# Attention by head pairs: two heads' scores on the two row halves of TensorE, their outputs on the two column halves, and VectorE on both heads at once

## The chip, the cores and the metric

The kernel runs on one core of one Trainium2 chip. The metric is the time of one execution on the device in microseconds. Three runs of the kernel before gave a median of 1569.54 us (1569.21 to 1569.62).

## The reference

Two model blocks are applied to 256 tokens of width 1024: the first has a gated-mixing layer, an attention layer and two feed-forward layers, the second three mixers and a mixture of 32 experts. The change touches only the attention core of the first block, with 16 heads of 64 elements. In the reference it is a softmax over three dilated patterns, merged by their log-sum-exp:

```python
for window, dilation in DILATED_PATTERNS:
    o, lse = dilated_branch(q, k, v, window, dilation)
...
wts = jax.nn.softmax(jnp.stack(lses, axis=0), axis=0)
return jnp.einsum('pbsh,pbshd->bshd', wts, jnp.stack(outs, axis=0))
```

For 256 tokens this equals one causal softmax whose score for a query and key has the logarithm of the number of patterns that hold the pair added to it, and that is how the kernel computes it: scores times 1/8 plus a table (`bias`), row maximum, exponential, sum, division, product with the values.

## The kernel before, in words

Tokens lie along the free axis, features on the partitions. There are two blocks of 128 query rows. The first sees 128 keys, the second all 256, so one head has 128 x 384 scores: a part c=0 of 128 columns and a part c=1 of 256. `qk1` holds queries and keys with two heads per tile, the even head on partitions 0 to 63 and the odd one on 64 to 127.

Each engine has its own program, in a fixed order written out by hand, and semaphores join them. In the attention loop (PE L990 to L1019, ScalarE L1574 to L1590, VectorE L2088 to L2112) each pass i deals with one head at different depths:

- PE: scores of head i (L996 and L997, into `mixbank(i)`, two PSUM banks in turn), after waiting until VectorE has read the scores of head i-2. After every odd head, one step of an unrelated vector-matrix product (`modulation`, L900: four matmuls of 512 columns, each on its own 32 columns of the array). Then three transposes of the probabilities of head i-2 (L1007), then three output matmuls of head i-3 (L1016 to L1018), whose 64 output rows lie on partition half i % 2 of `lin`.
- VectorE: scale and bias of head i (L2093), two row maxima (L2097), then reciprocal (L2102) and two multiplications (L2104) for head i-1, and in every even pass the split of a finished pair's outputs into `r_hi` and `r_lo` (`split_rows`, L1872 and L1873).
- ScalarE: two exponentials with their sums for head i (L1580), then the copy of the transposed probabilities of head i-2 from PSUM (L1588).

A VectorE pass i waits for outputs up to head i-3. PE computes these in its own pass i, ahead of which it needs the probabilities of head i-2, and those VectorE made in pass i-1, one pass earlier.

The loop starts when the last values are copied (L2084) and ends where `project` (L1022) multiplies all eight tiles of `r_hi` and `r_lo` by the output weights (L692 to L694). One `w_lo` split of a weight panel (L1848) stands in VectorE's order between the last two `split_rows`.

Of the kernel before, what the change touches and what calls it, by code (L numbers as in the profile page):

```python
# [24 lines left out]
ALU = mybir.AluOpType  # L25
ACT = mybir.ActivationFunctionType
AX = mybir.AxisListType.X
ds = bass.ds

P = 128  # L30
T = 256
NT = T // P
# [7 lines left out]
HEADS = 16  # L40
HD = 64
# [21 lines left out]
OUT1 = QKV1 + 3 * KD  # L63
# [119 lines left out]
def program(nc, A, out):  # L183
# [3 lines left out]
    with ctx:  # L187
# [27 lines left out]
        K, at = {}, 0  # L215
# [42 lines left out]
        lin = [ctx.enter_context(nc.psum_tensor(f"lin{b}", [P, 512], F32)) for b in range(4)]  # L258
        stat = ctx.enter_context(nc.psum_tensor("stat", [P, 4, T], F32))
        mixp = ctx.enter_context(nc.psum_tensor("mixp", [P, 4, T], F32))  # L260
# [41 lines left out]
        scores_ready = sem("scores_ready")  # L302
        scores_read = sem("scores_read")
        max_ready = sem("max_ready")
        exp_ready = sem("exp_ready")
        probs_ready = sem("probs_ready")
        pt_ready = sem("pt_ready")
        pt_copied = sem("pt_copied")
        o_ready = sem("o_ready")
        o_copied = sem("o_copied")  # L310
# [63 lines left out]
        low, a = Arena(moe_low, MOE_LOW), Arena(moe_high, MOE_HIGH)  # L374
# [82 lines left out]
        a = Arena(mixers_t, MIXERS)  # L457
# [12 lines left out]
        a = Arena(mixers_t, MIXERS)  # L470
        qk1 = a.take(16 * T).rearrange("p (k t) -> p k t", k=16)
# [4 lines left out]
        vt1 = a.take(NT * D).rearrange("p (c f) -> p c f", c=NT)  # L476
        SC = 3 * P
        s1 = a.take(4 * SC).rearrange("p (b s) -> p b s", b=4)
# [8 lines left out]
        def statbank(n):  # L487

            return stat[:, 2 * (n % 2):2 * (n % 2) + 2, :].rearrange("p a t -> p (a t)")

        def mixbank(n):

            return mixp[:, 2 * (n % 2):2 * (n % 2) + 2, :].rearrange("p a t -> p (a t)")
# [170 lines left out]
        def _(pe):  # L664
# [229 lines left out]
            def modulation(bank, first, count):  # L894

                for a in range(first, first + count):
                    k = a % KD
                    pe.wait_ge(ada_loaded[a % ARING], 16 * (a // ARING + 1))
                    for q in range(4):
                        mm = pe.matmul(bank[32 * q:32 * q + 32, :], c_act[:, k:k + 1].to_broadcast([P, 32]),  # L900
                                       aring[:, a % ARING, q * 512:(q + 1) * 512], start=k == 0, stop=k == KD - 1,
                                       skip_group_check=True)
                    mm.then_inc(ada_done, 1)
# [83 lines left out]
                mm.then_inc(vt1_ready, 1)  # L987
            pe.wait_ge(vt1_copied, 4)
            pe.wait_ge(qk_ready, 16)
            for i in range(HEADS + 3):  # L990
                if i < HEADS:
                    if i >= 2:
                        pe.wait_ge(scores_read, i - 1)
                    o = 64 * (i % 2)
                    q, k = qk1[o:o + 64, i // 2, :], qk1[o:o + 64, 8 + i // 2, :]
                    pe.matmul(mixbank(i)[:, 0:P], q[:, 0:P], k[:, 0:P], start=True, stop=True, skip_group_check=True)  # L996
                    pe.matmul(mixbank(i)[:, P:3 * P], q[:, P:T], k, start=True, stop=True, skip_group_check=True)\  # L997
                        .then_inc(scores_ready, 1)
                if i < HEADS and i % 2 == 1:
                    modulation(lin[2], 16 + i // 2, 1)  # L1000
                if 2 <= i <= HEADS + 1:
                    g = i - 2
                    pe.wait_ge(probs_ready, g + 1)
                    if g >= 2:
                        pe.wait_ge(pt_copied, g - 1)
                    for c in range(3):
                        mm = pe.transpose(statbank(g)[:, c * P:(c + 1) * P], p1[:, g % 4, c * P:(c + 1) * P], K["ident"])  # L1007
                    mm.then_inc(pt_ready, 1)
                if i >= 3:
                    g = i - 3  # L1010
                    pe.wait_ge(pt_copied, g + 1)
                    if g >= 4 and g % 2 == 0:
                        pe.wait_ge(o_copied, g // 2 - 1)
                    o = lin[(g // 2) % 2][64 * (g % 2):64 * (g % 2) + 64, :]
                    v = [vt1[:, c, g * HD:(g + 1) * HD] for c in range(NT)]
                    pe.matmul(o[:, 0:P], v[0], pt1[:, g % 4, 0:P], start=True, stop=True, skip_group_check=True)  # L1016
                    pe.matmul(o[:, P:T], v[0], pt1[:, g % 4, P:2 * P], start=True, stop=False, skip_group_check=True)
                    pe.matmul(o[:, P:T], v[1], pt1[:, g % 4, 2 * P:3 * P], start=False, stop=True, skip_group_check=True)\  # L1018
                        .then_inc(o_ready, 1)  # L1019
            pe.wait_ge(o_copied, 8)  # L1020
            pe.wait_ge(modrow_ready, 3)
            project((r_hi, r_lo))  # L1022
# [376 lines left out]
        def _(act):  # L1399
# [10 lines left out]
            def split_hi(upto):  # L1410

                for n in range(next_split[0], upto):
                    next_split[0] = n + 1
                    if is_split(n):
                        act.wait_ge(panel_loaded[n % RING], 16 * (n // RING + 1))
                        act.wait_ge(panel_done, n - RING + 1)
                        act.activation(w_hi[:, n % RING, :], ring[:, n % RING, :], ACT.Copy).then_inc(w_hi_ready, 1)  # L1417
# [152 lines left out]
            for n in range(8):  # L1570
                panels.done()
                panels.advance(1)
                split_hi(panels.n + RING)
            for i in range(HEADS + 2):  # L1574
                if i < HEADS:
                    act.wait_ge(max_ready, i + 1)
                    if i >= 4:
                        act.wait_ge(pt_ready, i - 3)
                    for c, (a0, a1) in enumerate(((0, P), (P, 3 * P))):
                        ins = act.activation(p1[:, i % 4, a0:a1], s1[:, i % 4, a0:a1], ACT.Exp,  # L1580
                                             bias=mx1[:, 2 * i + c:2 * i + c + 1], accum_out=l1[:, 2 * i + c:2 * i + c + 1])
                    ins.then_inc(exp_ready, 1)
                if i >= 2:
                    g = i - 2
                    act.wait_ge(pt_ready, g + 1)
                    if g >= 4:
                        act.wait_ge(o_ready, g - 3)
                    act.activation(pt1[:, g % 4, :], statbank(g)[:, 0:SC], ACT.Copy).then_inc(pt_copied, 1)  # L1588
                    if i == HEADS:
                        split_hi(OUT1 + 1)  # L1590
            split_hi(OUT1 + 4)
            modulation_row(lin[2][:, :], 2)
            stream_norm()
# [230 lines left out]
        def _(dve):  # L1824
# [3 lines left out]
            def link(ins):  # L1828

                ins.then_inc(dve_step, 1)  # L1830
                dve.wait_ge(dve_step, seen(dve_step))
# [38 lines left out]
            def split_rows(tiles, src):  # L1870

                link(dve.tensor_copy(r_hi[:, tiles, :], src))  # L1872
                return dve.tensor_tensor(r_lo[:, tiles, :], src, r_hi[:, tiles, :].bitcast(F32), ALU.subtract)  # L1873
# [211 lines left out]
            a0 = list(K).index("bias00")  # L2085
            bias_at = sum(v.shape[1] for v in list(consts.values())[:a0])
            bias = cst[:, bias_at:bias_at + SC]
            for i in range(HEADS + 3):  # L2088
                if i < HEADS:
                    dve.wait_ge(scores_ready, i + 1)  # L2090
                    if i >= 4:
                        dve.wait_ge(exp_ready, i - 3)
                    dve.scalar_tensor_tensor(s1[:, i % 4, :], mixbank(i)[:, 0:SC], HD ** -0.5, bias, ALU.mult, ALU.add)\  # L2093
                        .then_inc(scores_read, 1)
                    dve.wait_ge(scores_read, i + 1)
                    for c, (a0, a1) in enumerate(((0, P), (P, 3 * P))):
                        ins = dve.tensor_reduce(mx1[:, 2 * i + c:2 * i + c + 1], s1[:, i % 4, a0:a1], AX, ALU.max, negate=True)  # L2097
                    ins.then_inc(max_ready, 1)
                if 1 <= i <= HEADS:
                    g = i - 1  # L2100
                    dve.wait_ge(exp_ready, g + 1)
                    link(dve.reciprocal(r1[:, 2 * g:2 * g + 2], l1[:, 2 * g:2 * g + 2]))  # L2102
                    for c, (a0, a1) in enumerate(((0, P), (P, 3 * P))):
                        ins = dve.tensor_scalar(p1[:, g % 4, a0:a1], p1[:, g % 4, a0:a1], r1[:, 2 * g + c:2 * g + c + 1],  # L2104
                                                None, ALU.mult)
                    ins.then_inc(probs_ready, 1)
                if i >= 4 and i % 2 == 0:
                    j = (i - 4) // 2
                    dve.wait_ge(o_ready, 2 * j + 2)
                    split_rows(j, lin[j % 2][:, 0:T]).then_inc(o_copied, 1)  # L2110
                if i == HEADS + 1:
                    split_lo(OUT1 + 1)  # L2112
            split_lo(OUT1 + 4)
            residual(8)
# [498 lines left out]
```

## Time and profile before

| what | value |
|---|---|
| median of three runs | 1569.54 us |
| span of the profiled execution, first to last instruction | 1563.5 us |
| difference of the two | 6.0 us |
| PE busy over the span | 95% |
| VectorE, ScalarE, GpSimd busy | 50%, 37%, 19% |
| mean granted TensorE clock | 0.977 |
| attention loop, first score matmul to first matmul of `project` | 430.18 to 473.98 us |

The profile gives no total of its own for the profiled execution; the 6.0 us are what a median run has outside such a span. PE's busy share is modelled from its instructions and includes the time in which a half or a quarter of the array works. A granted clock of 1.00 is 2.4 GHz, 0.50 is 1.2 GHz.

### The profile page before, as it was taken

Reading aid. Unit: us, or ns where it says so; the run is one execution under the profiler, and the core shown is the slowest. Engines: PE = TensorE matmul, PEld = TensorE weight load, DVE = VectorE, ACT = ScalarE, POOL = GpSimd, SP = SyncE. Lnnn points to the kernel's source line nnn. Section 1 sums busy time; section 2 is a strip of 40 time slices with the busy share of each in tenths; the row PEclk is TensorE's granted clock in tenths of the full one; section 3 lists DMA queues with packets and bytes.
Section 4 is the critical chain, followed back from the end, with each engine's and each line's share of the span. In section 5 each row is a group of like instructions: output and inputs, shape, how many; then the busy total and the mean of one; then the engine's idle time right before and its main releaser. Section 6 shows DMA issues by size and latency. Waiting matters only on the chain.

```text
span 1563.5 us, 28411 instructions
## 1 busy us (share of the span) xinstructions
PE 1478.1 (95%) x11270; PEld 1234.4 (79%) x11270; DVE 777.1 (50%) x1404; ACT 573.0 (37%) x927; POOL 294.7 (19%) x121
## 2 busy tenths in 40 slices
PE   7978999999999999999999998999899999998997
PEld 5857999999958999999999887999566666555554
DVE  4964888648584888634463532572422222221122
ACT  2345545444354655437663113634211111111111
POOL 0021222212201112225763000684000000000000
PEclk9989999999999999998999996999999999999999
DMA  8674455565434555643543210476999999999996
GB/s 310 238 277 153 167 165 171 195 235 162 136 135 135 171 181 176 210 149 108 175 137 96 80 55 14 149 269 233 423 424 423 425 427 425 426 425 424 427 424 262
DMA packets 72097, 375.82 MB, mean 240 GB/s; under 512 B 8128, under 2 KB 8384, under 8 KB 49984
## 3 DMA queue, kind: packets, MB, share of 16 engines
q1 hardware_dynamic: 72000, 374.43, 63.5%
q8 instruction: 73, 1.20, 0.3%
q14 instruction: 24, 0.20, 0.0%
HBM read 373.35 MB, written 1.05 MB: 239 GB/s over the span
## 4 chain that ended last, share of the span: by engine, by line
PE 64%; issue 13%; DVE 8%; DMA 8%; SPq 5%; ACT 2%; POOL 1%; POOLq 0%; DVEq 0%; ACTq 0%
PE lin L692 9%; PE lin L694 8%; PE lin L693 8%; DMA moe_low<-in_experts 6%; PE stat L1376 5%; PE mixp L1349 4%; PE mixp L1353 4%; DVE mixers L2011 3%; SPq L609 3%; PE lin L711 2%; PE stat L1309 2%; PE lin L1319 1%; DMA moe_high<-in_experts 1%; PE stat L692 1%; PE stat L693 1%
## 5 line engine op out<-in xcount | busy, mean ns | idle before, releaser
L692 PE MATMUL lin<-r_hi,w_hi 128*128 128x256 f32 x1464 | 427.2, 292 | 12.0 <-POOL w_lo L1815 5.1
L693 PE MATMUL lin<-r_lo,w_hi 128*128 128x256 f32 x1464 | 417.4, 285 | 0.0
L694 PE MATMUL lin<-r_hi,w_lo 128*128 128x256 f32 x1464 | 417.3, 285 | 0.0
L692 PEld LDWEIGHTS lin<-r_hi,w_hi 128*128 128x128 f32 x1464 | 284.2, 194 | 19.6 <-POOL w_lo L1815 6.7
L693 PEld LDWEIGHTS lin<-r_lo,w_hi 128*128 128x128 f32 x1464 | 284.2, 194 | 0.8
L694 PEld LDWEIGHTS lin<-r_hi,w_lo 128*128 128x128 f32 x1464 | 284.1, 194 | 0.0
L1819 POOL TENSOR_TENSOR w_lo<-ring,w_hi 128x1024 fp32r<-128x1024 f32 x71 | 175.5, 2484 | 217.9 <-ACT w_hi L1417 217.7
L1815 POOL TENSOR_TENSOR w_lo<-ring,w_hi 128x1024 fp32r<-128x1024 f32 x42 | 108.2, 2577 | 481.5 <-ACT w_hi L1423 298.3
L1848 DVE TENSOR_TENSOR w_lo<-ring,w_hi 128x1024 fp32r<-128x1024 f32 x126 | 156.4, 1245 | 84.8 <-ACT w_hi L1423 65.1
L1423 ACT ACTIVATE w_hi<-ring 128x1024 fp32r<-128x1024 f32 x124 | 129.7, 1049 | 57.3 <-PE mixp L694 49.3
L1417 ACT ACTIVATE w_hi<-ring 128x1024 fp32r<-128x1024 f32 x119 | 124.0, 1050 | 33.8 <-PE lin L694 16.7
L2519 DVE TENSOR_TENSOR moe_low<-moe_low,mixp 128x256 f32<-128x256 f32 x32 | 13.5, 421 | 207.4 <-ACT moe_low L1789 207.4
L711 PE MATMUL lin<-h,ring 128*128 128x256 f32 x400 | 91.0, 385 | 3.0 <-DVE h L1879 3.0
L1789 ACT ACTIVATE moe_low<-mixp 128x256 f32<-128x256 f32 x32 | 12.3, 384 | 221.7 <-PE mixp L1353 221.7
L711 PEld LDWEIGHTS lin<-h,ring 128*128 128x128 f32 x400 | 76.1, 193 | 16.9 <-issue 6.7
L2526 DVE SCALAR_TENSOR_TENSOR e_y_lo<-stat,moe_high,e_y_hi 128x512 fp32r<-128x512 f32 x32 | 24.0, 751 | 117.3 <-ACT e_y_hi L1794 117.3
L1376 PE MATMUL stat<-moe_high,moe_low 128*64 128x512 f32 x352 | 80.4, 598 | 0.0
L1505 ACT ACTIVATE sgf<-ub 128x256 f32<-128x256 f32 x44 | 18.4, 418 | 119.0 <-DVE ub L1930 119.0
L1349 PE MATMUL mixp<-moe_low,h 128*64 128x256 f32 x352 | 53.3, 381 | 6.9 <-DMA moe_low<-in_experts 4.2
L1349 PE MATMUL mixp<-moe_low,cat 128*64 128x256 f32 x352 | 53.3, 381 | 5.9 <-DMA moe_high<-in_experts 3.5
L1376 PEld LDWEIGHTS stat<-moe_high,moe_low 128*64 128x64 f32 x352 | 23.2, 136 | 40.7 <-issue 37.8
L2011 DVE SCALAR_TENSOR_TENSOR mixers<-mixers,colp 128x256 f32<-128x256 f32 x120 | 53.9, 514 | 0.9
(482 smaller groups left out, 2773.7 us busy)
## 6 DMA issues: line engine op xcount, KB each, us to landing
ring<-in_panels SPq DMA_DIRECT2D x272, 512.0 KB, 3.9
moe_low<-in_experts SPq DMA_DIRECT2D x64, 1024.0 KB, 22.9
moe_high<-in_experts SPq DMA_DIRECT2D x22, 2048.0 KB, 24.9
aring<-in_ada SPq DMA_DIRECT2D x24, 1024.0 KB, 6.0
ring<-in_experts SPq DMA_DIRECT2D x20, 1024.0 KB, 26.9
moe_high<-in_experts SPq DMA_DIRECT2D x20, 1024.0 KB, 22.1
cst<-in_experts SPq DMA_DIRECT2D x10, 1280.0 KB, 23.8
sq<-in_experts SPq DMA_DIRECT2D x10, 1024.0 KB, 29.4
```

Source lines behind the costliest of these rows:

```text
L692: pe.matmul(o, w_hi[:, slot, c], r[0], start=start, stop=False, skip_group_check=True)
L693: pe.matmul(o, w_hi[:, slot, c], r[1], start=False, stop=False, skip_group_check=True)
L694: return pe.matmul(o, w_lo[:, slot, c], r[0], start=False, stop=stop, skip_group_check=True)
L711: mm = pe.matmul(lin[b][:, 0:T], w[:, i, :], rhs[:, i, :], start=i == 0, stop=i == k - 1)
L1349: pe.matmul(o[:, 0:T], lhs, gate_weights(slot, k)[:, half * T:(half + 1) * T], start=k == 0, stop=k == KD - 1, skip_group_check=True)
L1376: mm = pe.matmul(statbank(1)[64 * half:64 * half + 64, :], e_hidT[:, k % 2, k // 2, :], down_weights(slot, k, half), start=k == 0, stop=k ...
L1417: act.activation(w_hi[:, n % RING, :], ring[:, n % RING, :], ACT.Copy).then_inc(w_hi_ready, 1)
L1423: act.activation(w_hi[:, n % RING, :], ring[:, n % RING, :], ACT.Copy).then_inc(w_hi_ready, 1)
L1815: pool.tensor_tensor(w_lo[:, POOL_SLOT, :], ring[:, POOL_SLOT, :], w_hi[:, POOL_SLOT, :].bitcast(F32), ALU.subtract).then_inc(w_split_pool, 1)
L1819: pool.tensor_tensor(w_lo[:, n % RING, :], ring[:, n % RING, :], w_hi[:, n % RING, :].bitcast(F32), ALU.subtract).then_inc(w_split_pool, 1)
L1848: dve.tensor_tensor(w_lo[:, n % RING, :], ring[:, n % RING, :], w_hi[:, n % RING, :].bitcast(F32), ALU.subtract)\
L2011: ins = dve.scalar_tensor_tensor(cv0[:, j, :], hc0[:, j, tap:tap + T], w, cv0[:, j, :], ALU.mult, ALU.add)
```

## The change

PE, ScalarE and VectorE now take a pair of heads per pass, in nine or ten passes instead of 18 or 19.

- Scores: `score_pair(j)` issues c=0 of both heads, then c=1 of both, so that consecutive matmuls use the two halves of the array's rows and two PSUM banks. One pair fills both banks, and the next pair waits until VectorE has read them. `score_pair(j + 1)` stands first in PE's pass j, then `modulation`, then the six transposes of pair j-1, then the outputs of pair j-2.
- Outputs: for each of the three products both heads are issued one after the other, on the two column halves.
- VectorE: one scale-and-bias of 128 x 768, two maxima over both heads, one reciprocal of four columns, and two multiplications of both heads by a broadcast reciprocal (`tensor_tensor` in place of `tensor_scalar`). Pass j ends with `split_rows` of pair j-2, which waits for that pair's outputs.
- ScalarE: the same instructions, in pairs.
- The buffers stay at four heads, that is two pairs.

The removed lines are those of the kernel above; they are left out here.

```diff
--- before.py
+++ after.py
@@ -987,36 +987,46 @@
                 mm.then_inc(vt1_ready, 1)
             pe.wait_ge(vt1_copied, 4)
             pe.wait_ge(qk_ready, 16)
...
+            def score_pair(j):
+                if j:
+                    pe.wait_ge(scores_read, j)
+                for part in range(2):
+                    for n in range(2):
+                        q, k = (qk1[64 * n:64 * n + 64, t, :] for t in (j, 8 + j))
+                        if part == 0:
+                            pe.matmul(mixbank(n)[:, 0:P], q[:, 0:P], k[:, 0:P], start=True, stop=True, skip_group_check=True)
+                        else:
+                            mm = pe.matmul(mixbank(n)[:, P:3 * P], q[:, P:T], k, start=True, stop=True, skip_group_check=True)
+                mm.then_inc(scores_ready, 1)
+            score_pair(0)
+            for j in range(HEADS // 2 + 2):
+                if j + 1 < HEADS // 2:
+                    score_pair(j + 1)
+                if j < HEADS // 2:
+                    modulation(lin[2], 16 + j, 1)
+                if 1 <= j <= HEADS // 2:
+                    g = j - 1
                     pe.wait_ge(probs_ready, g + 1)
+                    for n in range(2):
+                        if g:
+                            pe.wait_ge(pt_copied, 2 * g - 1 + n)
+                        for c in range(3):
+                            mm = pe.transpose(statbank(n)[:, c * P:(c + 1) * P], p1[:, 2 * (g % 2) + n, c * P:(c + 1) * P], K["ident"])
+                        mm.then_inc(pt_ready, 1)
+                if j >= 2:
+                    g = j - 2
+                    pe.wait_ge(pt_copied, 2 * g + 2)
                     if g >= 2:
...
+                        pe.wait_ge(o_copied, g - 1)
                     for c in range(3):
...
+                        for n in range(2):
+                            head = 2 * g + n
+                            o = lin[g % 2][64 * n:64 * n + 64, (0 if c == 0 else P):(P if c == 0 else T)]
+                            mm = pe.matmul(o, vt1[:, c // 2, head * HD:(head + 1) * HD],
+                                           pt1[:, 2 * (g % 2) + n, c * P:(c + 1) * P], start=c < 2, stop=c != 1, skip_group_check=True)
+                    mm.then_inc(o_ready, 1)
             pe.wait_ge(o_copied, 8)
             pe.wait_ge(modrow_ready, 3)
             project((r_hi, r_lo))
@@ -1571,23 +1581,27 @@
                 panels.done()
                 panels.advance(1)
                 split_hi(panels.n + RING)
...
+            for j in range(HEADS // 2 + 1):
+                if j < HEADS // 2:
+                    act.wait_ge(max_ready, j + 1)
+                    if j >= 2:
+                        act.wait_ge(pt_ready, 2 * j - 2)
+                    for n in range(2):
+                        at = 2 * (j % 2) + n
+                        for c, (a0, a1) in enumerate(((0, P), (P, 3 * P))):
+                            m = 2 * (2 * j + n) + c
+                            ins = act.activation(p1[:, at, a0:a1], s1[:, at, a0:a1], ACT.Exp, bias=mx1[:, m:m + 1],
+                                                 accum_out=l1[:, m:m + 1])
                     ins.then_inc(exp_ready, 1)
...
+                if j:
+                    g = j - 1
+                    for n in range(2):
+                        act.wait_ge(pt_ready, 2 * g + n + 1)
+                        if g >= 2:
+                            act.wait_ge(o_ready, g - 1)
+                        act.activation(pt1[:, 2 * (g % 2) + n, :], statbank(n)[:, 0:SC], ACT.Copy).then_inc(pt_copied, 1)
+                if j == HEADS // 2 - 1:
+                    split_hi(OUT1 + 1)
             split_hi(OUT1 + 4)
             modulation_row(lin[2][:, :], 2)
             stream_norm()
@@ -2085,30 +2099,38 @@
             a0 = list(K).index("bias00")
             bias_at = sum(v.shape[1] for v in list(consts.values())[:a0])
             bias = cst[:, bias_at:bias_at + SC]
...
+            scores = mixp[:, :, :].rearrange("p (n a) t -> p n (a t)", n=2)[:, :, 0:SC]
+            def per_row(ap, j, c):
+                return ap[:, 4 * j:4 * j + 4].rearrange("p (n c) -> p n c", c=2)[:, :, c]
+            for j in range(HEADS // 2 + 2):
+                if j < HEADS // 2:
+                    pair = slice(2 * (j % 2), 2 * (j % 2) + 2)
+                    dve.wait_ge(scores_ready, j + 1)
+                    if j >= 2:
+                        dve.wait_ge(exp_ready, j - 1)
+                    dve.scalar_tensor_tensor(s1[:, pair, :], scores, HD ** -0.5, bias.unsqueeze(1).broadcast_to([P, 2, SC]),
+                                             ALU.mult, ALU.add).then_inc(scores_read, 1)
+                    dve.wait_ge(scores_read, j + 1)
                     for c, (a0, a1) in enumerate(((0, P), (P, 3 * P))):
...
+                        ins = dve.tensor_reduce(per_row(mx1, j, c), s1[:, pair, a0:a1], AX, ALU.max, negate=True)
                     ins.then_inc(max_ready, 1)
...
+                if 1 <= j <= HEADS // 2:
+                    g = j - 1
+                    pair = slice(2 * (g % 2), 2 * (g % 2) + 2)
                     dve.wait_ge(exp_ready, g + 1)
...
+                    link(dve.reciprocal(r1[:, 4 * g:4 * g + 4], l1[:, 4 * g:4 * g + 4]))
                     for c, (a0, a1) in enumerate(((0, P), (P, 3 * P))):
...
+                        ins = dve.tensor_tensor(p1[:, pair, a0:a1], p1[:, pair, a0:a1],
+                                                per_row(r1, g, c).unsqueeze(2).broadcast_to([P, 2, a1 - a0]), ALU.mult)
                     ins.then_inc(probs_ready, 1)
...
+                if j >= 2:
+                    g = j - 2
+                    dve.wait_ge(o_ready, g + 1)
+                    split_rows(g, lin[g % 2][:, 0:T]).then_inc(o_copied, 1)
+                if j == HEADS // 2:
                     split_lo(OUT1 + 1)
             split_lo(OUT1 + 4)
             residual(8)
```

## Rows read from the trace of the kernel before

**Rows 1.** Stretch, length, busy of PE, PEld, DVE, ACT, POOL, granted clock, DMA share, GB/s.

```profile
445.00:450.00 5.00, 5.00 (x35) 2.82 (x32) 4.00 (x14) 2.72 (x10) 0.00 (x0) 1.00 0.55 193
```

**Rows 2.** The chain of waits over one period of two heads: start, length, what.

```profile
440.84 0.99 PE lin L900 x8
441.84 0.48 PE stat L1007 x3
442.31 0.36 PE lin L1016 x2
442.68 0.22 PE lin L1017 x2
...
443.11 0.42 PE mixp L996 x2
443.53 0.43 PE mixp L997 x2
...
446.09 0.99 PE lin L900 x8
```

**Rows 3.** Timeline of PE: eight transposes, two heads' scores, first `project` matmul.

```profile
426.72 1.07 PE L985 MATMUL mixp<-cst,mixers 128*128 128x128 f32 x8 [0.56 <-issue]
...
430.18 0.50 PE L996 MATMUL mixp<-mixers 64*128 64x128 f32 x4 [0.78 <-DVE mixers L2084]
430.50 0.61 PE L997 MATMUL mixp<-mixers 64*128 64x256 f32 x4
...
473.98 0.39 PE L692 MATMUL lin<-r_hi,w_hi 128*128 128x256 f32 x1 [0.98 <-DVE r_lo L1873]
```

**Rows 4.** Timeline of VectorE: start, length, line; one head, then a split.

```profile
435.17 0.15 DVE L2102 RECIPROCAL mixers<-mixers 128x2 f32<-128x2 f32 x1
...
435.36 0.55 DVE L2104 TENSOR_SCALAR mixers<-mixers 128x128 f32<-128x128 f32 x2
...
435.82 0.55 DVE L2093 SCALAR_TENSOR_TENSOR mixers<-mixp,cst 128x384 f32<-128x384 f32 x1
436.41 0.61 DVE L2097 TENSOR_REDUCE mixers<-mixers 128x1 f32<-128x128 f32 x2
...
436.94 0.16 DVE L2102 RECIPROCAL mixers<-mixers 128x2 f32<-128x2 f32 x1
...
440.53 0.42 DVE L1872 CAST r_hi<-lin 128x256 fp32r<-128x256 f32 x1
...
440.98 0.42 DVE L1873 TENSOR_TENSOR r_lo<-lin,r_hi 128x256 fp32r<-128x256 f32 x1
```

**Rows 5.** VectorE by line and shape, whole run: count, busy us, mean ns, idle before.

```profile
L2375 DVE SCALAR_TENSOR_TENSOR arena<-stat,arena 128x768 f32<-128x768 f32 x1 | 0.9, 950 | 0.0
L2231 DVE TENSOR_TENSOR arena<-arena 128x512 f32<-128x512 f32 x2 | 1.3, 686 | 0.0
L2097 DVE TENSOR_REDUCE mixers<-mixers 128x1 f32<-128x256 f32 x16 | 6.5, 409 | 0.0
L2097 DVE TENSOR_REDUCE mixers<-mixers 128x1 f32<-128x128 f32 x16 | 4.6, 286 | 0.6
```

**Rows 6.** Timeline of PE in later stages: three matmul groups that followed an idle time (in brackets).

```profile
869.79 1.28 PE L1170 MATMUL stat<-cst,arena 128*128 128x128 f32 x8 [2.22 <-DVE arena L2296]
...
935.19 1.89 PE L1217 MATMUL mixp<-arena 64*128 64x128 f32 x8 [0.85 <-DVE arena L2333]
...
1425.51 0.65 PE L1349 MATMUL mixp<-ring,h 128*64 128x256 f32 x4 [1.69 <-DMA modrow<-in_experts]
```

**Rows 7.** Granted clock (third number from the end) around those three.

```profile
870.00:871.00 1.00, 1.00 (x9) 1.00 (x8) 1.00 (x2) 0.00 (x0) 0.00 (x0) 0.78 0.00 0
935.00:936.00 1.00, 0.81 (x4) 0.81 (x5) 0.14 (x1) 0.00 (x0) 0.00 (x0) 0.71 0.00 0
1420.00:1430.00 10.00, 8.31 (x80) 5.29 (x80) 1.11 (x2) 1.07 (x2) 0.00 (x0) 1.00 1.02 420
940.00:950.00 10.00, 7.86 (x30) 6.57 (x30) 1.81 (x5) 0.00 (x0) 0.00 (x0) 0.50 0.01 2
```

More of the change, by code:

```diff
@@ L989, in _ @@
             pe.wait_ge(qk_ready, 16)
[L990 to L1002, printed above, removed]
-                    pe.wait_ge(probs_ready, g + 1)
+            def score_pair(j):
[9 more added lines that the diff above has]
+                mm.then_inc(scores_ready, 1)
@@ L1004, in _ @@
                     if g >= 2:
-                        pe.wait_ge(pt_copied, g - 1)
+                        pe.wait_ge(o_copied, g - 1)
                     for c in range(3):
[L1007 to L1019, printed above, removed]
+                        for n in range(2):
[3 more added lines that the diff above has]
+                                           pt1[:, 2 * (g % 2) + n, c * P:(c + 1) * P], start=c < 2, stop=c != 1, skip_group_check=True)
@@ L1573, in _ @@
                 split_hi(panels.n + RING)
[L1574 to L1581, printed above, removed]
-                    ins.then_inc(exp_ready, 1)
[L1583 to L1590, printed above, removed]
+            for j in range(HEADS // 2 + 1):
[9 more added lines that the diff above has]
+                                                 accum_out=l1[:, m:m + 1])
+                    ins.then_inc(exp_ready, 1)
+                if j:
[7 more added lines that the diff above has]
+                    split_hi(OUT1 + 1)
             split_hi(OUT1 + 4)
@@ L2087, in _ @@
             bias = cst[:, bias_at:bias_at + SC]
[L2088 to L2095, printed above, removed]
+            scores = mixp[:, :, :].rearrange("p (n a) t -> p n (a t)", n=2)[:, :, 0:SC]
@@ L2096, in _ @@
                     for c, (a0, a1) in enumerate(((0, P), (P, 3 * P))):
-                        ins = dve.tensor_reduce(mx1[:, 2 * i + c:2 * i + c + 1], s1[:, i % 4, a0:a1], AX, ALU.max, negate=True)
+                        ins = dve.tensor_reduce(per_row(mx1, j, c), s1[:, pair, a0:a1], AX, ALU.max, negate=True)
                     ins.then_inc(max_ready, 1)
-                if 1 <= i <= HEADS:
-                    g = i - 1
+                if 1 <= j <= HEADS // 2:
+                    g = j - 1
+                    pair = slice(2 * (g % 2), 2 * (g % 2) + 2)
@@ L2101, in _ @@
                     dve.wait_ge(exp_ready, g + 1)
-                    link(dve.reciprocal(r1[:, 2 * g:2 * g + 2], l1[:, 2 * g:2 * g + 2]))
+                    link(dve.reciprocal(r1[:, 4 * g:4 * g + 4], l1[:, 4 * g:4 * g + 4]))
                     for c, (a0, a1) in enumerate(((0, P), (P, 3 * P))):
-                        ins = dve.tensor_scalar(p1[:, g % 4, a0:a1], p1[:, g % 4, a0:a1], r1[:, 2 * g + c:2 * g + c + 1],
-                                                None, ALU.mult)
+                        ins = dve.tensor_tensor(p1[:, pair, a0:a1], p1[:, pair, a0:a1],
+                                                per_row(r1, g, c).unsqueeze(2).broadcast_to([P, 2, a1 - a0]), ALU.mult)
@@ L2106, in _ @@
                     ins.then_inc(probs_ready, 1)
[L2107 to L2111, printed above, removed]
+                if j >= 2:
[3 more added lines that the diff above has]
+                if j == HEADS // 2:
```

## The prediction

> **What bounds the kernel now.** I read the chain of waits over the attention loop first. It runs through PE alone, with the same pieces in every period of two heads, 440.84 to 446.09, that is 5.25 us: one `modulation` at 0.99, then twice (transposes 0.48, outputs 0.36 + 0.22 + 0.22 = 0.80, scores 0.42 + 0.43 = 0.85) [rows 2]; 0.99 + 2 x 2.13 = 5.25. The busy times by stretch say the same: PE 5.00 of 5.00 us, VectorE 4.00, ScalarE 2.72, clock 1.00 [rows 1]. A product of 128 columns takes 0.22 once the array streams; the first of a group takes 0.36 or 0.42, so each change from one tile shape to the next costs 0.14 to 0.21. The `modulation` row shows that column tiles already work side by side: four matmuls of 512 columns in 0.99 us, where one after the other, at 0.43 for 256 columns, they would need 3.4. The row halves do too: two heads' scores together ran from 430.18 to 431.11, 0.93 us, where their columns add up to 2 x 0.65 [rows 2, 3].
>
> **PE's own work after.** Per pair: scores 0.21 + 0.22 + 0.43, about 0.85; `modulation` 0.99; six transposes, by eight that took 1.07 [rows 3], 0.86; outputs 0.80. Sum 3.50 instead of 5.25. Two thirds of the saving is the second head riding along (1.3), the rest fewer changes of shape.
>
> **VectorE's own work after.** Where no wait lies between, an instruction starts 0.09 before the previous one's end (0.55 long, the next after 0.46), and after a semaphore 0.04 to 0.05 behind it [rows 4].
> - Scale and bias over 768 elements: 0.95 by a row of that shape [rows 5], plus 0.05: 1.00.
> - Maxima: from 286 to 409 ns for 128 more elements [rows 5], so 0.41 for 256 and 0.65 for 512 elements; start to next start 0.32 + 0.57 = 0.89 (two heads singly: 2 x 0.53).
> - Reciprocal to multiplication: 0.19 [rows 4], taken as 0.20.
> - Multiplications. No row shows one with a broadcast factor. The old form takes 0.55 for both parts of one head; a `tensor_tensor` takes 0.42 for 256 and 0.69 for 512 elements [rows 4, 5], which gives 0.33 + 0.69 = 1.02 to the end. That is the value I take. Bounds: the slope of the old form would give about 0.73, twice one head 1.10.
> - Split: copy to subtraction 0.45, subtraction 0.42 less 0.09 [rows 4]: 0.78 before the next can start.
>
> Together 3.8 us per pair (0.94 for the multiplications when nothing waits on their end), hardly less than the 2 x 1.79 + 0.78 = 4.4 of before. If both engines only had to do their work, the period would be 3.8.
>
> **The added wait.** But VectorE's pass j ends with the split of pair j-2, whose outputs PE computes in its pass j behind the transposes of pair j-1, and these need the multiplications of VectorE's same pass j. Before, the probabilities came from one pass earlier, so that slack is gone. Queued behind the waiting split are the scale of pair j+1, the maxima, and so ScalarE's exponentials, and PE's scores of pair j+2, whose banks that scale has to free. So the two engines take turns:
>
> 1.00 (scale) + 0.89 (maxima) + 0.20 (reciprocal) + 1.02 (multiply, to its end) + 0.05 + 0.86 (six transposes) + 0.80 (outputs) + 0.04 + 0.78 (split) = 5.64 us per pair, against 5.25.
>
> What hides: scores and `modulation`, 0.85 + 0.99 from 0.05 after the scale, end at 2.9 and the probabilities come at 3.1. ScalarE's exponentials (2 x 0.9) and two copies (0.9), 2.7 in all by its busy time per period [rows 1], fit behind the maxima and ahead of the next outputs. Bounds of the cycle: transposes 0.80 to 0.97, the multiplications as above, 5.3 to 5.9.
>
> **Whole loop at full clock.** Scores from 430.18, scale 0 at 431.04, scale 1 at 432.9 (its banks), scale 2 at 436.1 (waits for the exponentials, 1.9 us, then multiplies; no split yet), scale 3 at 441.8 (first full cycle), then 5.64 each: scale 7 at 464.3. Split of pair 5 ends at 469.9; multiplications 7 end 471.1; transposes and outputs of pair 6 until 472.9, its split until 473.7; the `w_lo` split that stands there 1.1; last split 0.87; `project` starts about 475.8, against 473.98 [rows 3]. That is +1.8 us: the first passes win what the later cycles lose. The move of `w_hi` work on ScalarE costs nothing, since its engine is idle half the time [rows 1]. The later stages follow unchanged, and so do the 6.0 us that a median run has outside the span of the profiled one.
>
> **The clock.** Before, PE never rested in the loop and the clock stayed at 1.00. After, from the end of the outputs to the next scores PE rests for split + scale, 0.04 + 0.78 + 1.00 + 0.05 = 1.9 us, in each of the five full cycles, and another 0.2 ahead of the transposes. In this trace a rest of 1.69 us between dense groups left the clock at 1.00, one of 2.22 was followed by 0.50 (the row of 870 shows 0.78, the change within it), and so were two of 0.85 close together among small matmuls on half the rows or columns, at 935; that stretch then stayed at 0.50 for about 30 us [rows 6, 7]. A rest of 1.9 every 5.6 us, with small matmuls between, resembles these more than the first. I take it that the clock falls to 1.2 GHz. The Trainium skill, "TensorE: Matmul & The Clock Gate", section on a second failure mode, says that a kernel that idles briefly between groups of matmuls while it cycles through PSUM makes the clock swing between its two levels; by that rule too the clock falls, where the rests alone would not decide.
>
> Price at 1.2 GHz: scores and `modulation` grow by 0.64 + 0.85 and end at 4.4, so the transposes wait 1.3 longer; transposes and outputs grow by 0.6 + 0.6. A cycle at the low clock costs 2.5 more, 8.1. At the low clock PE is busier and should win the clock back, then lose it again; I take half of the five full cycles, 2.5 x 2.5 = 6.2. `project` may begin at the low clock, which I leave within the range (a few us of dense work at half rate). Sum: 1.8 + 6.2 = +8.0, so 1577.5.
>
> A rule that speaks against the change is in the skill's "TensorEngine Tiling (Array Packing)", section on the PSUM bottleneck: tiling speeds up TensorE but not the reading of PSUM. The trace agrees: VectorE's 3.8 above PE's 3.5.
>
> **Rivals.**
> - The clock holds at 2.4 GHz. For: 1.9 is nearer to 1.69 than to 2.22, and PE is busy for two thirds of the cycle. Against: the fall at 935 with shorter rests. Time 1569.5 + 1.8 = 1571.3 (1569 to 1574). 28%.
> - Faster: VectorE doesn't wait for the outputs, and its 3.8 us set the pace. This needs the split to find its outputs done; it decides once transposes and outputs are finished when the multiplications end. Seven periods would save 7 x (5.25 - 3.8) = 10, so 1559.5. Against it stands PE's written order. 5%.
> - The clock falls and does not come back, as after 935 [rows 7]. All five cycles at +2.5, the first and last passes and the opening of `project` some 4 more: 1.8 + 12.5 + 4, so 1588. 8%.
> - The change does not do what it says: halves don't run side by side when issued alternately. Outputs +0.64, and scores +0.64 of which 0.4 shows, 1.0 a cycle, 1.8 + 7 x 1.0, so 1578. Against: rows 2 and 3. 4%.
>
> **How the numbers follow.** Forecast 55%, own range 1573 to 1583. Less than 0.2%, 3.1 us, can't be told from no change. Faster than that: the second rival and a hair of the first, 6%. Within it: most of the first rival and the low end of the forecast, 27%. Slower 67%. The range reaches down over the first rival and up short of the third: 1569.5 to 1584.
>
> **What would show it.** VectorE's wait before the split's copy should be released by PE's outputs, some 1.75 us in each pass from the third on, and PE's before the scores by the scale, 1.9 us. The period should be 5.6 at clock 1.00 and about 8 at 0.50; the granted clock of 440 to 475 says which case holds. Outputs of a pair in 0.8 us show the column halves side by side. The forecast is wrong if that clock stays at 1.00, or if the split finds its outputs ready.

## The result and the profile after

The changed kernel took 1576.56 us (median of 4 runs, 1575.65 to 1577.92) against 1569.58 us for the kernel before (also 4 runs); the ratio is 1.0047, 95% interval 1.0033 to 1.0061. It is slower, 0.9 us from the forecast of 1577.5. The profiled execution took 1575.65 us with a span of 1573.9 us, so 1.8 us lie outside the span, not the 6.0 taken before.

From the first score matmul (431.34) to the first matmul of `project` (484.19) the attention loop took 52.9 us, against 43.8 [rows 3]: 9.1 us more, while the medians differ by 7.0. Loops are compared this way below, because what lies ahead of and behind the loop is not the same in every execution: span less loop was 1515.4 us in one profile of this document (e8) and 1524.9 in another (e5), and 1519.7 before and 1521.0 after the change. The 2 us between 9.1 and 7.0 are within that and stay unexplained.

These two lines stand at the head of the changed kernel's page; VectorE is busy a little less than before (777.1 us), although the kernel is longer:

```profile
span 1573.9 us, 28344 instructions
...
PE 1473.2 (94%) x11270; PEld 1229.4 (78%) x11270; DVE 771.7 (49%) x1356; ACT 573.1 (36%) x927; POOL 295.3 (19%) x121
```

The chain of waits over one period of two heads, the answer to [rows 2]: start, length, what.

```profile
449.31 0.44 DVE r_hi L1886
449.80 0.31 issue
450.11 0.96 DVE mixers L2114
451.11 0.49 PE mixp L998 x4
451.60 0.76 PE mixp L1000 x4
452.36 1.86 PE lin L900 x8
454.23 1.19 PE stat L1016 x6
455.42 0.83 PE lin L1027 x12
456.27 0.43 DVE r_hi L1886
```

The chain was PE alone; now it passes from VectorE (split, scale) to PE (scores, `modulation`, transposes, outputs) and back, in 456.27 - 449.31 = 6.96 us instead of 5.25. `modulation` takes 1.86 instead of 0.99, though it is the same eight instructions. The stretches of one us say why (behind the bounds and the length stands PE's busy time; the granted clock is the third number from the end):

```profile
449.00:450.00 1.00, 0.26 (x6) 0.01 (x2) 0.66 (x2) 0.00 (x0) 0.00 (x0) 1.00 0.90 369
450.00:451.00 1.00, 0.00 (x0) 0.00 (x0) 1.00 (x2) 0.00 (x0) 0.00 (x0) 1.00 0.95 401
451.00:452.00 1.00, 0.89 (x8) 0.54 (x8) 0.97 (x3) 0.00 (x0) 0.00 (x0) 0.79 0.32 131
452.00:453.00 1.00, 1.00 (x6) 0.20 (x8) 0.97 (x4) 0.86 (x4) 0.00 (x0) 0.50 0.00 0
453.00:454.00 1.00, 1.00 (x8) 0.00 (x0) 0.25 (x1) 1.00 (x6) 0.00 (x0) 0.50 0.00 0
454.00:455.00 1.00, 1.00 (x8) 0.84 (x5) 0.00 (x0) 0.00 (x0) 0.00 (x0) 0.51 0.00 0
455.00:456.00 1.00, 1.00 (x16) 0.81 (x14) 0.00 (x0) 0.87 (x2) 0.00 (x0) 1.00 0.74 98
```

PE rests from 449.26 to 451.11, works again, and is put to 1.2 GHz (0.50) within the same us; it returns to 2.4 GHz while the transposes run. Four full periods in a row look like this; the one ahead of them, from scale to scale 443.14 - 437.40 = 5.74 us, ran wholly at 1.00:

```profile
437.40 0.95 DVE L2114 SCALAR_TENSOR_TENSOR mixers<-mixp,cst 128x768 f32<-128x768 f32 x1
...
443.14 0.95 DVE L2114 SCALAR_TENSOR_TENSOR mixers<-mixp,cst 128x768 f32<-128x768 f32 x1
```

The timeline has the rest as an idle time in brackets, and VectorE's wait for the outputs:

```profile
451.11 0.49 PE L998 MATMUL mixp<-mixers 64*128 64x128 f32 x4 [1.85 <-DVE mixers L2114]
```

```profile
449.31 0.42 DVE L1886 CAST r_hi<-lin 128x256 fp32r<-128x256 f32 x1 [3.02 <-PE lin L1027]
```

### The profile page after: what moved, and what is told of

The parts are those of the page before. It is cut to its first block, busy times and chain, and to the rows that moved or that the text cites. A ratio compares the mean times of both kernels' runs of the same rounds, so it can differ in the third digit from the quotient of the medians.

```text
span 1573.9 us, 28344 instructions
## 1 busy us (share of the span) xinstructions
PE 1473.2 (94%) x11270; PEld 1229.4 (78%) x11270; DVE 771.7 (49%) x1356; ACT 573.1 (36%) x927; POOL 295.3 (19%) x121
## 4 chain that ended last, share of the span: by engine, by line
PE 61%; issue 13%; DVE 9%; DMA 7%; SPq 7%; ACT 2%; POOL 1%; POOLq 0%; DVEq 0%; ACTq 0%
PE lin L692 8%; PE lin L694 8%; PE lin L693 8%; DMA moe_low<-in_experts 5%; PE stat L1386 4%; PE mixp L1359 4%; PE mixp L1363 4%; SPq L609 3%; DVE mixers L2025 3%; PE lin L711 2%; PE stat L1319 2%; DMA moe_high<-in_experts 1%; PE lin L1329 1%; PE stat L692 1%; PE mixp L692 1%
```

## The experiments

Each experiment was measured in turn with the kernel before, whose median was 1569.3 us beside e1 to e4, 1569.2 beside e5 to e8, 1569.4 beside e9 to e11 and 1569.6 beside the changed kernel; each ratio is to its own one. The loop runs from the first score matmul to the first matmul of `project`; the period is the time per pair of heads in the middle of the loop. Both come from the one profiled execution of each kernel.

| kernel | median us | ratio, 95% interval | loop us | period us |
|---|---|---|---|---|
| before | 1569.3 | 1 | 43.8 | 5.25 |
| changed | 1576.6 | 1.0047 (1.0033 to 1.0061) | 52.9 | 6.96 |
| e1 fill | 1572.0 | 1.0023 (1.0009 to 1.0037) | 46.3 | 5.72 |
| e2 late split | 1556.3 | 0.9911 (0.9898 to 0.9924) | 33.2 | 3.85 |
| e3 modulation last | 1569.8 | 1.0001 (0.9989 to 1.0012) | 48.6 | 5.72, 7.06 |
| e4 fill, head by head | 1573.4 | 1.0033 (1.0017 to 1.0049) | 48.7 | 5.98 |
| e5 old kernel, added wait | 1577.1 | 1.0046 (1.0028 to 1.0064) | 54.3 | 6.48 |
| e6 late split, ScalarE rounds | 1551.8 | 0.9877 (0.9858 to 0.9896) | 31.7 | 3.47 |
| e7 late split, VectorE single | 1559.0 | 0.9930 (0.9916 to 0.9944) | 34.5 | 4.02 |
| e8 late split, PE head by head | 1557.3 | 0.9918 (0.9904 to 0.9931) | 33.9 | 3.85 |
| e9 = e6 again | 1555.5 | 0.9890 (0.9867 to 0.9913) | 31.7 | 3.47 |
| e10 = e6, PE head by head | 1556.5 | 0.9910 (0.9894 to 0.9927) | 33.3 | 3.74 |
| e11 = e6, VectorE single | 1556.1 | 0.9910 (0.9887 to 0.9933) | 32.5 | 3.55 |

**e1, the rest filled.** Behind the outputs of passes 2 to 6:

```diff
+                    if j < HEADS // 2 - 1:
+                        for _ in range(3):
+                            pe.matmul(lin[3][:, 0:T], K["ident"], cst[:, 0:T], ...)
```

> The changed kernel with three extra matmuls of 256 columns (about 1.3 us, into a bank nobody reads) behind the outputs of passes 2 to 6, where TensorE rests 1.9 us. Theory (VectorE and TensorE take turns at 5.6 us a pair, and the rest of 1.9 us drops the clock, which adds 1.3 us a pair): clock 1.00 in the whole loop, period 5.6 us instead of 6.97, about 1569.6 + 1.8 = 1571.4 us. Rival 1 (the low clock only goes along with the loss, the period is long for another reason): period near 7, 1576.5 us as before the fill. Rival 2 (the turn-taking costs nothing at full clock): period 5.25 or less, 1569.5 us or below.

The clock stayed at 1.00 from 430 to 484 and the period is 5.72. The chain of waits over one period:

```profile
449.93 0.43 DVE r_hi L1889
450.42 0.31 issue
450.73 0.96 DVE mixers L2117
451.71 1.01 DVE mixers L2121 x2
452.84 1.04 DVE mixers L2129 x2
453.92 0.88 PE stat L1016 x6
454.80 0.83 PE lin L1027 x12
455.65 0.43 DVE r_hi L1889
```

This is the turn-taking by itself: split, scale, maxima, multiplications, transposes, outputs, each engine idle while the other works. Extra work made the kernel faster by 6.6 us in the loop and 4.6 in the median; the intervals of the two ratios overlap at their ends, so the loop carries this verdict. Rival 1 is out, and so is rival 2, since 5.72 is above 5.25 and the interval above 1. The 12 runs spread from 1567.9 to 1578.7; the last passes have no fill, and one profile can't show whether the clock falls there in some executions.

**e2, the wait removed.** VectorE splits pair j-3 in pass j:

```diff
-            for j in range(HEADS // 2 + 2):
+            for j in range(HEADS // 2 + 3):
...
-                if j >= 2:
-                    g = j - 2
+                if j >= 3:
+                    g = j - 3
```

> The changed kernel with VectorE's split of a pair's outputs one pass later (pair j-3 in pass j, one pass more), so that it no longer waits for outputs that depend on its own pass's multiplications. Theory (the added wait makes the two engines take turns): the wait is gone, VectorE's work of 3.8 us sets the period, TensorE rests too little for the clock to fall, and the loop ends some 10 us before that of the old kernel: 1559.5 us (1557 to 1562). Rival 1 (PSUM banks and transposed copies form the next cycle at once): period 4.5 to 5.2, 1563 to 1569 us. Rival 2 (the loss came from the pairing itself, wide VectorE instructions and tile changes): no gain over the changed kernel, 1574 to 1577 us.

VectorE no longer waits; the chain is VectorE alone, 452.49 - 448.64 = 3.85 us a pair, as its work was summed (3.8), and the clock is 1.00 throughout the loop. The loop is 10.6 us shorter than the old one (10 expected), the median 13.0 shorter. Both rivals fail.

```profile
448.64 0.96 DVE mixers L2114
449.62 1.01 DVE mixers L2118 x2
450.75 1.03 DVE mixers L2126 x2
451.78 0.34 DVE r_hi L1886
452.18 0.31 issue
452.49 0.96 DVE mixers L2114
```

**e3, the long rest cut in two.** `modulation` moved behind the outputs:

```diff
+                if j < HEADS // 2:
+                    modulation(lin[2], 16 + j, 1)
```

> The changed kernel with the modulation step moved from behind the scores to the end of TensorE's pass, into the long rest. The rest of 1.9 us becomes one of 0.9 us, and one of about 1.2 us opens ahead of the transposes; the work and VectorE's turn-taking stay. If the clock falls for one long rest, it now stays at 1.00 and the time is that of the filled kernel, about 1571.5 us. If it falls for the sum of rests within a few us, it falls as before; the modulation then runs at the low clock off the path, so the period is 6 to 7 us and the time 1574 to 1577 us.

Neither answer came out clean. Four of the five full periods kept 1.00 and took 5.72 us, one took 7.06, and the clock also fell in an early pass and in the last ones; the runs spread from 1564.7 to 1574.1, and the profiled one is at the slow end. The fall in the middle of the loop came behind two short rests:

```profile
457.98 0.49 PE L998 MATMUL mixp<-mixers 64*128 64x128 f32 x4 [0.85 <-DVE mixers L2114]
458.30 0.60 PE L1000 MATMUL mixp<-mixers 64*128 64x256 f32 x4
460.17 1.11 PE L1014 MATMUL stat<-cst,mixers 128*128 128x128 f32 x4 [1.27 <-DVE mixers L2126]
```

```profile
460.00:461.00 1.00, 0.83 (x4) 0.83 (x5) 0.11 (x1) 0.87 (x4) 0.00 (x0) 0.54 1.04 442
```

So no single long rest is needed; rests of 0.85 and 1.27 us with 0.9 us of matmuls between were followed by a fall once, and the same pattern one period earlier was not. The median, 1569.8, lies below the 1571.5 expected for a clock that holds; no profile shows why.

**e4, outputs head by head at full clock.** e1 with the loops over c and n swapped.

> The filled kernel with the outputs head by head (three products of the even head, then three of the odd one) instead of alternating between the column halves. Theory (halves overlap between neighbouring matmuls alone): five slots of 0.21 us instead of three, +0.43 us a pair on the path, outputs 1.25 us, about 3 us over the filled kernel. Rival (the queue overlaps the halves however they are ordered): no difference. Rival (nothing overlaps in this order): 1.45 us, +0.64 a pair, about 5 us over.

Outputs took 1.09 us instead of 0.83, less than the 1.25 expected: +0.26 a pair, period 5.98. The median is 1.4 us above e1 with intervals that overlap; the loop is 2.4 longer, 1.6 of it by 0.26 in each of six passes and the rest in the last passes, where the clock fell (0.50 from 477.1 to 480.5 in this profile).

```profile
454.77 1.09 PE lin L1027 x12
```

**e5, the added wait alone, in the old kernel.**

```diff
-                if i >= 4 and i % 2 == 0:
-                    j = (i - 4) // 2
+                if i >= 3 and i % 2 == 1:
+                    j = (i - 3) // 2
```

> The kernel before, one head a pass and everything as it was, with only VectorE's split of a finished pair moved one pass earlier (odd passes from the third), so that it waits for outputs that need the probabilities of its own pass: the added wait alone, without pairs. Theory (the wait is what costs): VectorE's 4.4 us for two heads plus a wait for three transposes and three outputs, 0.05 + 0.5 + 0.8, and some time lost when TensorE in its turn waits for scales: 5.7 to 6.2 us per two heads instead of 5.25, 1573 to 1577 us if the clock holds, more if it falls. Rival (the loss belongs to the paired form): period 5.25, 1569.3 us.

No pair, no wide instruction, no alternation, and the same loss: 1577.1 us, period 457.15 - 450.67 = 6.48. The period is longer than expected, since the outputs also wait for ScalarE's copies, which stand behind its exponentials; and it is at clock 1.00 (450 to 460), so here the wait costs by itself, in the median, what in the changed kernel wait and clock cost together. The profiled execution took 1581.0 us, and its loop is 10.5 us longer than the old one. The edit has a side effect at the end: the `w_lo` split now stands behind the last `split_rows`, PE rests 2.31 us ahead of `project`, and that began at 0.50 (488 to 491), so a part of this profile's loss lies behind the loop.

```profile
449.87 0.43 DVE r_hi L1872
450.37 0.31 issue
450.67 0.56 DVE mixers L2093
451.25 0.62 DVE mixers L2097 x2
...
452.21 0.68 ACT mixers L1580 x3
452.89 0.38 ACT mixers L1588
453.31 0.43 PE lin L1016 x2
...
457.15 0.56 DVE mixers L2093
```

**e6 and e9, ScalarE takes the rounding.** e2 with the copy to `r_hi` on ScalarE, ahead of the exponentials of its pass:

```diff
+                if j >= 3:
+                    g = j - 3
+                    act.wait_ge(o_ready, g + 1)
+                    act.activation(r_hi[:, g, :], lin[g % 2][:, 0:T], ACT.Copy).then_inc(v_scaled, 1)
```

> The kernel with the late split, with ScalarE making the rounded upper part of the outputs ahead of its exponentials, VectorE only the subtraction. If VectorE's work is the bound of that kernel (3.85 us a pair), its 0.45 us less bring the period to TensorE's 3.5 to 3.6 us and the time 1.5 to 2 us below the late split, about 1554.5 us. Rival (the chain scale, maxima, exponentials, multiplications is the bound): the added 0.45 us on ScalarE delays the exponentials and the time is the same or up to 2 us longer.

> The kernel with the late split and ScalarE's share once more, since its first four runs lay far apart (1548.5 to 1557.7). If its gain is the shorter loop (31.7 us from the first scores to the projection in its profile, against 43.8), the median comes out near 1569.3 - 12.1 = 1557; if more than the loop is gained, near 1552 again.

PE alone is on the chain again, 450.37 - 446.90 = 3.47 us a pair, the 3.5 summed for its work (profile of e9):

```profile
446.90 0.42 PE mixp L998 x4
447.32 0.43 PE mixp L1000 x4
447.76 0.99 PE lin L900 x8
448.75 0.81 PE stat L1016 x6
449.56 0.81 PE lin L1027 x12
450.37 0.42 PE mixp L998 x4
```

The loop is 12.1 us shorter than the old one in both profiles. The medians are 17.4 and 13.9 us lower, with intervals that overlap; the ten runs of both together have a median of 1553.8 us, 15.5 lower. What goes beyond the loop's 12.1 is not explained: the two fastest runs of e9 (1547.5 and 1548.5) had a mean granted clock of 0.981 and 0.982, its others 0.975 to 0.978, so the spread is in part one of the clock elsewhere. Against e2 the loop gains 1.5 us; the medians of e2 and e9, 0.9 apart, don't separate them. Its loop is the shortest of all, and it is ahead of both given kernels.

**e7 and e8, one part of the change taken out of e2.** e7: two scales, four maxima and four TENSOR_SCALAR multiplications per pair. e8: scores and outputs head by head within the pass.

> The kernel with the late split, with VectorE's scale, maxima and multiplications head by head again (two, four and four instructions of the old shapes, TENSOR_SCALAR for the multiplication), TensorE in pairs. It takes away only the third part of the change, both heads at once on VectorE. By the rows of the old kernel the work grows from 3.85 to about 4.05 us a pair: +1.5 us in all, about 1558 us. If wide instructions were what makes the late split fast, the period would go back towards 4.4 or 5.2, 1561 to 1567 us.

> The kernel with the late split, with the scores and the outputs issued head by head within the pass instead of alternately: takes away only the alternation. TensorE's work grows by 0.13 (scores) and 0.26 (outputs, as in the filled kernel) to 3.9 us a pair, just VectorE's 3.85: same time or up to 1.5 us more, 1556 to 1558 us. If neighbouring matmuls on opposite halves are what gives the speed, outputs at 1.44 and scores at 1.28: 4.6 us a pair, 1562 us.

In e7 a pair takes 4.02 us instead of 3.85, and the loop 1.3 more: wide VectorE instructions are worth 0.17 us a pair where VectorE is the bound. Its median is 2.6 above e2's, with intervals that overlap. In e8 the period is the same and the median 0.9 higher, which can't be told from no change: in the steady period the alternation is worth nothing where VectorE is the bound. The outputs took 0.26 longer as expected, but the scores no longer, where 0.13 had been expected. The loop is 0.6 longer; in this profile the clock was at 0.50 from 430.5 to 433.9, in the first passes, where in e2 it was not, and what each of the two did to those 0.6 can't be told apart.

**e10 and e11, the same two parts taken out of e6**, where PE is the bound.

> The same kernel with scores and outputs head by head within a pass. TensorE sets its period (3.47 us), so here the alternation must show where it works: outputs 1.07 instead of 0.81 and scores the same, 3.7 us a pair, +2 us in all. If alternation did nothing: no change. If the halves overlap only when alternated (scores too): 3.47 + 0.64 + 0.43 = 4.5, +7 us.

> The same kernel with VectorE head by head (old shapes). VectorE's work is 3.85 - 0.45 + 0.16 = 3.6 us a pair by the profiles of the late-split kernels, TensorE's 3.47: +0.1 us a pair, within 1 us of the kernel with pairs. If the wide instructions matter more: +0.5 us a pair, +4 us.

In e10 a pair takes 3.74 us and the loop 1.6 more. All but 0.01 of the 0.27 a pair is in the outputs (1.07 against 0.81); the scores take 0.43 + 0.43 against 0.42 + 0.43. In e11 a pair takes 3.55 us and the loop 0.8 more. The medians lie 1.0 and 0.6 above e9, inside the intervals; the loops carry these two verdicts.

```profile
447.01 1.07 PE lin L1027 x12
448.09 0.43 PE mixp L998 x4
448.51 0.43 PE mixp L1000 x4
```

## Why the prediction was right, step by step

- **The added wait.** This was right, and it is shown from both sides: without the wait the changed kernel gains 20 us (e2), and with it the old kernel loses 8 (e5). VectorE was to wait 1.75 us for the outputs; it waited 1.79 in the first full cycle, at 1.00, and 3.02 in those where the clock fell.
- **The cycle of 5.64 us at full clock.** It took 5.72 in e1 and 5.74 in the changed kernel's first full cycle. In e1 (forecast in brackets) the transposes took 0.88 (0.86), the outputs 0.83 (0.80), scale to the next instruction 0.98 (1.00), maxima and reciprocal 1.13 (0.89 + 0.20). The 0.08 are made of such small pieces.
- **PE's own 3.50, VectorE's 3.8.** These measured 3.47 in e6 and 3.85 in e2. The second head riding along, 1.3 of the 1.75 saved, is three quarters of the saving and not two thirds; nothing hangs on it.
- **The multiplication with a broadcast factor.** I took it at the price of an ordinary `tensor_tensor`, 0.42 and 0.69 us [rows 4, 5]; it took 424 and 684 ns.
- **The first passes win, the later lose, +1.8 at full clock.** With the clock held, in e1, it was +2.5 in the loop and +2.7 in the median.
- **The clock falls.** The direction was right: 0.50 within each of four full periods, each time behind a rest of 1.85 (1.9 forecast; the one ahead of the transposes was 0.28 at full clock). That the price came near is in part luck. I took five cycles with a rest ahead of the scores, half of them at the low clock for their whole length at 2.5 us each. There were four (no scores follow the fifth), each at the low clock for about half of its length, and each cost 6.96 - 5.72 = 1.24, so 5.0 together; the period was never the 8 that I named as the sign of the low clock. Another 1.6 came in the last two passes, at 0.50 from 475.5 to 482.3, which the sum had at nothing. Together that is 52.9 - 46.3 = 6.6 between the loops without and with the fill, against 6.2 forecast. `project` began at 1.00, so nothing was due there.
- **Outside the span.** The 6.0 us were a mistake of reading. Every run with both numbers on record, before and after the change, has 1.7 to 1.9 us outside its span. So the span of 1563.5 belonged to an execution some 4 us under the median, by this estimate. The sum wasn't hurt, because it was a difference inside the loop.
- **The size.** The loop lost 9.1 us against 8.0 forecast, the median 7.0; the two errors of about 1 us have opposite signs.
- **The Trainium skill's two rules.** The Trainium skill, "TensorEngine Tiling (Array Packing)", section on the PSUM bottleneck, says that tiling makes TensorE faster but not the reading of PSUM. In e2 VectorE does set the pace with 3.85 us, but only its scale and its split read PSUM, 0.98 + 0.79 of the 3.85. The runs so show a bound by VectorE's whole work, by a margin that one 0.45 us read of PSUM moved to ScalarE turned round (e6); the forecast's "the trace agrees" says more than its 3.8 against 3.5 can. The Trainium skill, "TensorE: Matmul & The Clock Gate", section on a second failure mode, has the clock swing between its two levels in a kernel with frequent short idle times between groups of matmuls (its case is bf16 with 512 columns, this one fp32). The stretches of one us agree, 1.00 to 0.50 and back in four periods. The rule alone would not have decided, since e5 has such rests too (0.90 and 0.19 us in a period of 6.48) and its loop stayed at 1.00.

Where the expected gain of pairing went: it is real, 1.75 us of PE's work per pair (5.25 to 3.5), and e6 has it. In the changed kernel it became rests, since the split was placed in the one pass whose outputs can't be ready.

## What to carry to other kernels

When two or more steps of a software pipeline are merged into one pass, every distance counted in passes keeps its number but is checked anew: a consumer that had one pass of slack here had none afterwards, and that cost more than the merged work saved (at full clock 5.72 - 3.85 = 1.87 us a pair, against 5.25 - 3.85 = 1.40). Before making an engine's work shorter, walk once round the loop and ask what each wait needs from the same pass. And where PE must rest in each period, look at the granted clock as well: the rest may be paid a second time.

## What the runs showed that was not expected

- Useless matmuls in a rest made the kernel faster: 3 x 0.43 us of them in five passes, 6.6 us off the loop.
- The fall and the return of the clock went in step with the loop: four periods of 6.96 us alike, about half of each at 0.50.
- Row halves overlap without alternation: from the first matmul to VectorE's scale, both heads' scores took 0.97 us alternated (431.34 to 432.31) and 0.99 head by head (e8, 427.77 to 428.76). Column halves overlap partly head by head: 1.09 against 0.83 us.
- With the same instructions, executions of e3 lay up to 9.4 us apart, those of e1 10.9, and those of e11 11.8, although e11's profile has 1.00 through its whole loop. So much of this spread does not come from the loop: ahead of 430 us the granted clock was at 0.50 for about 14 us in the profile of e8 and for about 27 us in that of e2, and their loops began at 427.8 and 435.7. One profile is one draw.
